# Memory projections in wider matmuls: values over 512 weight columns, keys with high and low memory side by side

## What is computed

```python
for l in range(DEPTH):                                   # DEPTH = 2
    mk = (mem_prompt @ w_ck[l]).reshape(Bp, N_MEM, H_X, D_X)     # 256 tokens, 4 heads, 256 channels a head
    mv = (mem_prompt @ w_cv[l]).reshape(Bp, N_MEM, H_X, D_X)
    xp, ... = trunk_layer(xp, l, lp, rel_bias, mk, mv, ...)      # p_mem_k, p_mem_v are mk, mv of both layers
# in trunk_layer, the cross-attention:
    s = jnp.einsum('bqhd,bkhd->bhqk', qc, mem_k) * (D_X ** -0.5)
    p = jax.nn.softmax(s, axis=-1)
    x = x + jnp.einsum('bhqk,bkhd->bqhd', p, mem_v).reshape(B, L, H_X * D_X) @ w_co
```

## Time and profile before

| | us |
|---|---|
| median of 3 runs | 1917.35 |
| lowest and highest run | 1912.59, 1920.39 |
| span of the profiled execution | 1913.9 |
| TensorE busy in it | 1833.7 |
| VectorE busy | 967.8 |
| ScalarE busy | 589.2 |

### The profile page before, as it was taken

How to read it: one execution, slowest core, us unless ns; L and a number is a source line. 1 busy time by engine, 2 the same in 40 slices (tenths; PEclk the granted TensorE clock), 3 DMA queues, 4 the chain that set the end, 5 groups by cost and what they waited for, 6 DMA issues and landing times. The chain is left out here.

```text
span 1913.9 us, 35113 instructions
## 1 busy us (share of the span) xinstructions
PE 1833.7 (96%) x14681; PEld 1743.8 (91%) x14681; DVE 967.8 (51%) x2170; ACT 589.2 (31%) x1051; POOL 2.2 (0%) x7
## 2 busy tenths in 40 slices
PE   6998999999999999999989899999999999999997
PEld 5988888998899999999979788899988999999996
DVE  4565667544454434434545637765444443343345
ACT  4221345323332212212322114443234222222233
POOL 0000000000000000000000000000000000000000
PEclk9999999999999999999989989999999999999998
DMA  5313323322323233332232332242241233233222
GB/s 161 85 51 54 79 71 112 116 76 84 98 73 96 89 89 89 89 88 84 73 85 67 50 66 73 81 142 78 77 128 56 79 89 98 78 89 98 79 83 86
DMA packets 303475, 164.64 MB, mean 86 GB/s; under 512 B 16121, under 2 KB 299721, under 8 KB 303309
## 3 DMA queue, kind: packets, MB, share of 16 engines
q1 hardware_dynamic: 303308, 162.29, 30.1%
HBM read 151.07 MB, written 11.16 MB: 85 GB/s over the span
## 5 line engine op out<-in xcount | busy, mean ns | idle before, releaser
L911 PE MATMUL proj<-xg_hi,w_hi 128*128 128x272 f32 x1664 | 446.2, 287 | 0.0
L910 PE MATMUL proj<-xg_lo,w_hi 128*128 128x272 f32 x1664 | 445.9, 287 | 0.0
L1350 DVE TENSOR_TENSOR w_lo<-raw,w_hi 128x1024 fp32r<-128x1024 f32 (+1 forms) x268 | 323.0, 1205 | 125.8 <-ACT w_hi L1165 125.0
L910 PE MATMUL proj<-xn_lo,w_hi 128*128 128x272 f32 x1376 | 375.5, 291 | 0.0
L911 PE MATMUL proj<-xn_hi,w_hi 128*128 128x272 f32 x1376 | 374.5, 291 | 0.0
L908 PE MATMUL proj<-xg_hi,w_lo 128*128 128x272 f32 x1664 | 346.6, 290 | 0.0
L1165 ACT ACTIVATE w_hi<-raw 128x1024 fp32r<-128x1024 f32 (+1 forms) x268 | 276.7, 1037 | 176.3 <-PE proj L911 171.9
L908 PE MATMUL proj<-xn_hi,w_lo 128*128 128x272 f32 x1376 | 298.4, 299 | 19.0 <-DVE w_lo L1345 16.4
L910 PEld LDWEIGHTS proj<-xg_lo,w_hi 128*128 128x128 f32 x1664 | 313.1, 188 | 0.0
L911 PEld LDWEIGHTS proj<-xg_hi,w_hi 128*128 128x128 f32 x1664 | 313.0, 188 | 0.0
L910 PEld LDWEIGHTS proj<-xn_lo,w_hi 128*128 128x128 f32 x1376 | 263.9, 192 | 0.0
(11 more groups left out here) (320 smaller groups left out, 1974.7 us busy)
## 6 DMA issues: line engine op xcount, KB each, us to landing
raw<-in_w_in SPq DMA_DIRECT2D x54, 512.0 KB, 3.7
raw<-in_w_gate SPq DMA_DIRECT2D x44, 512.0 KB, 3.8
raw<-in_w_up SPq DMA_DIRECT2D x44, 512.0 KB, 3.8
raw<-in_w_down SPq DMA_DIRECT2D x32, 512.0 KB, 3.6
raw<-in_w_ck SPq DMA_DIRECT2D x16, 512.0 KB, 3.6
raw<-in_w_cv SPq DMA_DIRECT2D x16, 512.0 KB, 3.5
raw<-in_w_out SPq DMA_DIRECT2D x16, 512.0 KB, 3.6
raw<-in_w_cq SPq DMA_DIRECT2D x16, 512.0 KB, 3.5
```

Source lines behind the costliest of these rows:

```text
L910: mm(pb[h][:, 0:HALF], wh, xl[:, a:b], start=False, stop=False)
L911: last = mm(pb[h][:, 0:HALF], wh, xh[:, a:b], start=False, stop=final)
L1350: v.tensor_tensor(w_lo[:, s, 0:nt, :], raw[:, r, 0:nt, :], w_hi[:, s, 0:nt, :].bitcast(F32), ALU.subtract).then_inc(split_lo, 1)
```

## The change

It has three parts.

- **Values.** A `cv` tile now covers 512 weight columns (`CV_W`), so there are two tiles a layer instead of four. Each is made of four units of 2 blocks by 512 columns, and a unit is 12 matmuls of 512 columns instead of 24 of 256. ScalarE copies 512 columns per half of the tokens.
- **Keys.** `mem_hi` and `mem_lo` become halves of one buffer `mem`. For each block one matmul multiplies the high weights with high and low memory side by side, 512 columns into a whole bank, and a second one of 256 columns adds low weights x high memory onto the half of the low product. ScalarE copies that half to `mkT` and signals `mk_half`; VectorE then adds the other half from PSUM (L1361 of the new file), and this frees the bank.
- **Order.** With the tiles of values changed, the filler lists change. In the attention the four units of `cv0` stand where `cv0`, `ck2` and `ck3` stood, and `ck2` and `ck3` where `cv1` stood. In the cross-attention `ck6` takes the place of `cv2` in the first head, the four units of `cv1` stand in the second head, and `ck7` ends the third, where the second unit of `cv3` was.

The diff, cut to what is spoken of:

```diff
-            ("ck", 1), ("cv", 0), ("ck", 2), ("ck", 3), ("cv", 1)]
+            ("ck", 1), ("cv", 0), ("ck", 2), ("ck", 3)]
 TAIL_FILL = [("ck", 4), ("ck", 5)]
-CROSS_FILL = [[("cq", 2), ("cq", 3), ("cv", 2)], [("cq", 4), ("cq", 5), ("ck", 6), ("ck", 7)],
-              [("cq", 6), ("cq", 7), ("cv", 3)]]
+CROSS_FILL = [[("cq", 2), ("cq", 3), ("ck", 6)], [("cq", 4), ("cq", 5), ("cv", 1)],
+              [("cq", 6), ("cq", 7), ("ck", 7)]]
...
         elif kind == "cv":
-            parts, m = [("w_cv", 0, KT // 2, 2 * P * j, 0), ("w_cv", KT // 2, KT // 2, 2 * P * j, KT // 2)], 2 * P
+            parts, m = [("w_cv", 2 * q, 2, CV_W * j, 2 * q) for q in range(KT // 2)], CV_W
...
-            items += [(f, 0)] if f[0] == "ck" else [(f, 0), (f, 1)]
+            items += [(f, part) for part in range({"ck": 1, "cv": KT // 2}.get(f[0], 2))]
...
-        mem_hi = sb("mem_hi", [P, KT, N_MEM], F32R)
-        mem_lo = sb("mem_lo", [P, KT, N_MEM], F32R)
+        mem = sb("mem", [P, 2, KT, N_MEM], F32R)
+        mem_hi, mem_lo = mem[:, 0], mem[:, 1]
...
                             if kind == "cv":
-                                wh, wl = wide(w_hi[:, n % NHL])[:, k, :], wide(w_lo[:, n % NHL])[:, k, :]
+                                wh, wl = wide(w_hi[:, n % NHL], CV_W)[:, k, :], wide(w_lo[:, n % NHL], CV_W)[:, k, :]
                                 for tt in range(2):
-                                    o, c = pb[tt][:, 0:2 * P], slice(P * tt, P * tt + P)
+                                    o, c = pb[tt][:, 0:CV_W], slice(P * tt, P * tt + P)
...
                             elif kind == "ck":
-                                o = pb[0][:, 0:N_MEM]
-                                mm(o, wl, xh, start=first, stop=False)
-                                mm(o, wh, xl, start=False, stop=False)
-                                last = mm(o, wh, xh, start=False, stop=final)
+                                both = pb[0][:].rearrange("p (n t) -> p n t", n=2)
+                                mm(both, wh, mem[:, :, u["k0"] + k, :], start=first, stop=False)
+                                last = mm(pb[0][:, N_MEM:2 * N_MEM], wl, xh, start=False, stop=final)
...
                         if kind == "ck":
                             act.wait_ge(unit_done, n + 1)
-                            af(mkT[:, j, :], proj[u["slot"]][0][:, 0:N_MEM], ACT.Copy).then_inc(slot_free[u["slot"]], 1)
+                            af(mkT[:, j, :], proj[u["slot"]][0][:, N_MEM:2 * N_MEM], ACT.Copy).then_inc(mk_half, 1)
...
-                        if not u["last"] or kind in ("ck", "cv"):
+                        if not u["last"] or kind == "cv":
+                            return
+                        if kind == "ck":
+                            dve.wait_ge(mk_half, j + 1)
+                            v.tensor_tensor(mkT[:, j, :], mkT[:, j, :], proj[s][0][:, 0:N_MEM], ALU.add).then_inc(slot_free[s], 1)
                             return
```

More of the change, by code:

```diff
@@ L49 @@
 N_FF = -(-FT // HID)
+CV_W = 512
 DOWN = [f"down{f}" for f in range(N_FF)]
@@ L151, in weave @@
                 f, half = items[done]
-                first = len(units) if half == 0 else made[f][1][1][0] if f[0] == "cv" else None
+                first = len(units) if half == 0 else made[f][half][1][0] if f[0] == "cv" else None
                 if first is not None:
@@ L496, in hybrid_streaming_encoder_step @@
         unit_done = sem("unit_done")
+        mk_half = sem("mk_half")
         slot_free = [sem(f"slot_free{s}") for s in range(2)]
@@ L522, in hybrid_streaming_encoder_step @@
         own_dve, own_act = sem("own_dve"), sem("own_act")
-        sems = [*raw_in, split_hi, split_lo, unit_done, *slot_free, *full, *free, params_in, bias_in, rows_spread,
+        sems = [*raw_in, split_hi, split_lo, unit_done, mk_half, *slot_free, *full, *free, params_in, bias_in, rows_spread,
                 root_ready, xn_hi_s, xn_lo_s, xg_hi_s, xg_lo_s, sq_ready, sq_added, head_sq, pads_set, o_sig,
@@ L554, in memory_stored, with wide @@
             e.wait_ge(mv_stored, 16)
-        def wide(w):
-            return w.rearrange("p k c -> p (k c)").rearrange("p (k c) -> p k c", c=2 * P)
+        def wide(w, m):
+            return w.rearrange("p k c -> p (k c)").rearrange("p (k c) -> p k c", c=m)
         def token_sums(pe, bank, x, columns):
@@ L743, in weights @@
                             w = of(u["w"]).rearrange("l (k p) n -> p (l k) n", p=P)
-                            dst = wide(raw[:, r]) if u["m"] > P else raw[:, r, 0:u["nk"], 0:u["m"]]
+                            dst = wide(raw[:, r], u["m"]) if u["m"] > P else raw[:, r, 0:u["nk"], 0:u["m"]]
                             load(dst, w[:, u["r0"]:u["r0"] + u["nk"], u["c0"]:u["c0"] + u["m"]], raw_in[r])
@@ L807, in _ @@
                                 n_stored += 4
-                            if u["kind"] == "cv" and u["j"] == H_X - 1:
-                                tile_read(sp, "cv", H_X - 1)
-                                tile_read(sp, "cv", H_X - 2)
+                            if u["kind"] == "cv" and u["j"] == D // CV_W - 1:
+                                for n in range(D // CV_W):
+                                    tile_read(sp, "cv", n)
                                 load(to("p_mem_v").rearrange("l b (t p) h d -> p (l b t) (h d)", p=P), mv[:], mv_stored)
@@ L1177, in evacuate @@
                             for tt in range(2):
-                                af(mv[:, tt, D_X * j:D_X * j + D_X], proj[u["slot"]][tt][:, 0:D_X], ACT.Copy).then_inc(slot_free[u["slot"]], 1)
+                                af(mv[:, tt, CV_W * j:CV_W * j + CV_W], proj[u["slot"]][tt][:, 0:CV_W], ACT.Copy).then_inc(slot_free[u["slot"]], 1)
                         elif (kind, j) == ("o", 1):
```

## The result

The changed kernel takes 1928.12 us in the median of 11 runs (1922.63 to 1935.69), the kernel before 1917.0 us (11 runs, 1906.16 to 1923.46). The ratio is 1.0055, with a 95% interval of 1.0033 to 1.0076: slower by 6 to 15 us. In a later series, with 6 runs of it, it is 1.0064 (1.0046 to 1.0083). The forecast was 1920.6, the range 1911 to 1928: the measured time lies on its upper edge.

The account below looks back on a forecast made before the run. The prediction took TensorE as the bound: -4.7 us net matmul saving plus waits of 2.0, 3.8 and 2.1 gave +3.2 on 1917.35, so 1920.6 us. The range was 1911 to 1928 us.

Parts of the forecast that it names:

- TensorE sets the pace, and waits are paid in full: Whole kernel: TensorE busy 96% of 1913.9 us, so matmul time saved shortens it and added waits lengthen it fully.
- a few us in all: TensorE's list of waits in the kernel before: apart from start and layer changes, it was said to wait only this much.
- The waits: New TensorE waits: 2.0 us at `mk_turn` 2 and 3, 3.8 around `mk_turn` 1, 2.1 behind `ck0`.
- 0.41 us for the addition: VectorE's new 128x256 addition behind each key tile: estimated length, from a 272-column row of 0.433 us; handover 0.1 more.
- The saving of the wide matmul: Memory projections: 512-column matmuls save 1.7 us a layer on values, 1.1 on keys, 5.7 us in two layers.
- I take 0.222: Time in us of a rounded 512-column matmul, chosen between 0.226 and the fp32 lower bound of 0.216.
- 0.226: Time in us of a 512-column matmul if the 0.013 us excess stays once per instruction; saving then 4.4 us.
- The lost part of the saving: Three units a layer after which TensorE waits anyway: 0.5 us a layer, 1.0 us of the saving lost, 4.7 left.
- Covered additions and the new order of the cross-attention cost nothing: Additions behind `ck1` and `ck6`, and moved units between cross-attention phases: costed at nothing; additions 2 us at most if uncovered.
- slower rival: Memory projections: excess belongs to the columns, 512 take 0.240 us or more, no saving pays the waits: 1925.3 us; chance 0.14.
- faster rival: Wide matmuls take 0.216 us and additions are mostly covered, `ck0`'s costing nothing: -2.6 us, 1914.8 us; chance 0.18.
- much faster one: Wide matmuls at the Trainium skill's sustained 131 ns spacing: 29 us less than at 0.222, about 1891 us; chance 0.01.

Follow-up runs that it names:

- e3_turns_later: Changed kernel with `mk_turn` 1 and 2 moved later and `ck7` first filler of the third head, a phase before `mk_turn` 3: 1910.52 us, 0.9979 of the kernel before.
- e2_values_only: Changed kernel with its value tiles and order, but keys in three 256-column matmuls and one copy as before: 1915.65 us, 1.0013 of the kernel before.
- e1_keys_only: Kernel before with only the key part of the change, in the old order and with the old value tiles: 1920.37 us against 1914.12, ratio 1.0030.
- e7_all_waits_filled: Changed kernel with unused matmuls filling five TensorE waits a layer (`mk_turn` 1 to 3, `a_mix` (3,4), `x_keys` 3): 1919.76 us, 1.0036 of the kernel before.

## Why the prediction was right and wrong

The forecast of no difference beyond 0.5% was just missed by the median ratio of 1.0055, whose interval goes to both sides of that mark; a slowdown of 3.2 us was forecast and one of 11 came. That the time still lies at the edge of the range is luck: the range had been widened for the scatter of the runs, not for the term that was missing. Most steps held, and two failed.

- **TensorE sets the pace, and waits are paid in full.** Held. Covering the waits (`e3_turns_later`) took all of the loss away. But "a few us in all" was misread: the same list has, behind no start and no layer change, two idle times for which the profile names no releaser, with the clock down around them. Such idle times of 1.5 us and more stand in every trace, in the mLSTM or the projections beside it, 4.6 to 15.1 us in sum and different in two traces of one kernel (13.0 and 10.8 for the changed one). The change doesn't touch them. They may be one reason for the scatter of whole runs, and what makes them no run here tells. In the kernel before:

```profile
PE work L1031 <- issue: 7.7, 1, 7.7
...
PE work L1028 <- issue: 5.0, 1, 5.0
```

- **The waits.** Held nearly to the tenth: forecast +7.9 us. Measured 6.1 - 2.3 = 3.8 for `mkT`, 1.7 for `mk_st`, 1.9 in two layers behind `ck0`: +7.4. The 0.41 us for the addition was 0.42.
- **The saving of the wide matmul.** Mis-sized: the step "I take 0.222". It is 0.229 for values and 0.23 for keys. So the excess beside the columns stays with the instruction, as 0.226 would have had it, and grows a little with width: 0.013 us at 256 columns, 0.016 at 512. The fp32 matmul that holds the array as long was the wrong neighbour; the rounded matmuls of the earlier trace rows were the right one. By these spacings the saving is 192 x 0.011 + 128 x 0.013 = 3.8 us and not 5.7. Over whole units it is less still: from the first to the last start a value unit went from 2.834 to 2.606 us and a key unit from 2.837 to 2.767 (medians of the 15 or 16 units at the upper clock). With the last matmul that is 0.12 and 0.07 us a unit, 16 units each: 3.0 us. The bound from the Trainium skill, "TensorE: Matmul & The Clock Gate", Back-to-back issue gap (N/2.4 + 2.5 ns, 216 ns here), isn't reached by the rounded matmuls of 512 columns in this case, which start 0.229 us apart, and its 131 ns are ruled out by the same spacing.
- **The lost part of the saving.** 0.3 to 0.4 us a layer by the same reasoning, in place of 0.5. The first layer from attention to `f_sum` 3 came out 2.9 us longer; waits (3.3) less the saving there (0.8 by the spacings) give 2.5.
- **Covered additions and the new order of the cross-attention cost nothing.** Nearly held: the waits behind `ck1` and `ck6` don't exist, nor is there a wait for `w_lo` in the parts of `cv1`. From the cross norm to the next one the second layer, with the clock up in both, takes 164.57 us before and 164.66 now (first two rows before, last two rows now, below). Of the difference of +0.1 the longer wait of `mk_turn` 3 is +0.45 and the shorter units -0.6, so about 0.2 us a layer are left for the order. `e2_values_only`, which has the order but no additions, shows the same (164.29, where its units alone would give 164.1). `e1_keys_only`, which has the additions in the old order, has none of it (164.88 measured and by its terms).

```profile
1330.49 0.69 PE L564 MATMUL work<-ones,ssum 128*128 128x1 f32 x5 [0.69 <-DVE ssum L1494]
1495.06 0.47 PE L564 MATMUL work<-ones,ssum 128*128 128x1 f32 x3 [0.67 <-DVE ssum L1494]
```

```profile
1344.11 0.35 PE L566 MATMUL work<-ones,ssum 128*128 128x1 f32 x2 [0.69 <-DVE ssum L1499]
1508.77 0.47 PE L566 MATMUL work<-ones,ssum 128*128 128x1 f32 x3 [0.69 <-DVE ssum L1499]
```

- **What was left out: the clock.** I had costed a wait at its own length, and what stands behind it at nothing. Behind the longer waits of `mk_turn` 1, 2 and 3 the clock falls. That is 10 to 16 us more at the lower level in the mean of the runs, at half their length 5 to 8 us, the largest item after the waits themselves. By `e7_all_waits_filled` it is 4.9 us (1.3 to 8.5), by the stretches of the two traces 4.1.

Sum: +7.4 in waits, -3.8 + 0.8 for the matmuls, +5 for the clock: +9.4 of the 11 measured. Of the rest the smaller saving over whole units is 0.8 us and the order of the cross-attention 0.4. The stretches agree: 2.9 us a layer more from the attention to `f_sum` 3 and 0.1 in the cross-attention are 6.0, with the clock up, and with 5 for the clock 11.

The slower rival came nearest in time (1925.3), but for a reason that isn't the one: its 0.240 us is wrong, and the kernel is slower although the matmul came out at 0.229. The faster rival fell with the waits, which are all there, and the much faster one with the spacing.

## What to carry to other kernels

When TensorE is the bound, cost a wait that is added to it twice: its length, and what the clock may lose behind it, as here, where waits of 0.85 to 1.0 us stand close together. Read the granted clock of the stretch behind the waits, not only of the wait. A step that is split over two engines (copy, then add) needs its consumer one phase later; if the consumer stays where it was, the handover lands on the critical path. And for the price of an operation that the trace lacks, take the neighbour of the same number format and extrapolate it, rather than one of another format that happens to last as long.

## What the runs showed of the hardware

- In a run of rounded (fp32r) matmuls, each with its own weight load, one costs 0.120 us at 256 columns, 0.1256 at 272 and 0.229 at 512, at the upper clock: 0.012 to 0.016 us beside its columns. The first spacing of most units is 0.08 to 0.11 us longer, at 256 columns (0.20 to 0.22) and at 512 (0.31 to 0.34). Plain fp32 matmuls show 0.002 to 0.003.
- A matmul of 512 columns read as two runs of 256 from different places (the keys, 0.23 us) is no dearer than one with a contiguous run (0.229) to within 0.005 us.
- Work that nobody needs, put into TensorE's waits, made the kernel faster by 4.9 us (1.3 to 8.5). The stretches at the lower clock behind these waits, three in each of the two traces of the changed kernel, were gone in its trace.
